# Streams' attention of a two-layer encoder: both head groups in one unit, and W_out prepared beside it

## The reference, cut to what matters

```python
def _mla_attend(q_lat, q_rope, ckv, kr, mask):
    s = (jnp.einsum('bqhl,bkl->bhqk', q_lat, ckv).astype(jnp.float32)
         + jnp.einsum('bqhr,bkr->bhqk', q_rope, kr).astype(jnp.float32)) * MLA_SCALE
    ...
    p = jax.nn.softmax(s, axis=-1).astype(ckv.dtype)
    return jnp.einsum('bhqk,bkl->bqhl', p, ckv)
...
    mix = jnp.concatenate([rms_norm(o_a, g_a), rms_norm(o_swa, g_b)], axis=-1)
    x = layer_norm(ALPHA * x + jnp.einsum('btm,md->btd', mix, w_out), ln1_g, ln1_b)
```

## Time and profile before

| | us |
|---|---|
| median of three runs | 3708.36 (3703.28 to 3713.0) |
| the profiled execution | 3722.36, of which span 3720.5 |
| phase E, layer 0 and layer 1, with its barrier | 197.5 and 196.0 |
| from E's last matmul to the first W_out matmul, layer 0 | 786.7 to 834.9 |
| C from there on | about 147 |
| mean granted TensorE clock of the execution | 0.904 |

### The profile page before, as it was taken

How to read it: one execution, slowest core, us unless ns; L and a number is a source line. 1 busy time by engine, 2 the same in 40 slices (tenths; PEclk the granted TensorE clock), 3 DMA queues, 4 the chain that set the end, 5 groups by cost and what they waited for, 6 DMA issues and landing times. The chain is left out here.

```text
span 3720.5 us, 47086 instructions
## 1 busy us (share of the span) xinstructions
PE 3187.4 (86%) x18498; PEld 2906.4 (78%) x18498; DVE 1675.4 (45%) x3072; ACT 868.9 (23%) x1684; POOL 706.3 (19%) x627
## 2 busy tenths in 40 slices
PE   1978887749899999999859688878598999999995
PEld 1966665747799999999749566657478999999995
DVE  5456775635522322223354577756363322223226
ACT  1323332522311111111123223334223111111111
POOL 1222332001112112211012133310111112121111
PEclk9988897659999999999869789966699999999997
DMA  5320113321211101110133110042322101111001
GB/s 188 100 68 26 29 32 83 101 102 68 70 45 39 39 34 51 39 45 23 49 106 109 50 32 29 24 107 72 112 69 75 40 34 51 40 41 38 34 23 63
DMA packets 118134, 221.32 MB, mean 59 GB/s; under 512 B 33280, under 2 KB 70688, under 8 KB 117296
## 3 DMA queue, kind: packets, MB, share of 16 engines
q1 hardware_dynamic: 106752, 185.43, 15.5%
q0 software_dynamic: 11248, 34.09, 2.4%
HBM read 179.36 MB, written 42.46 MB: 60 GB/s over the span
## 5 line engine op out<-in xcount | busy, mean ns | idle before, releaser
L2131 PE MATMUL PS<-xh,fwh 128*128 128x390 f32 (+1 forms) x2112 | 718.7, 340 | 7.1 <-DVE fwl L2075 7.1
L2132 PE MATMUL PS<-xl,fwh 128*128 128x390 f32 (+1 forms) x2112 | 722.6, 342 | 0.0
L2133 PE MATMUL PS<-xh,fwl 128*128 128x390 f32 (+1 forms) x2112 | 721.8, 342 | 0.0
L2099 DVE TENSOR_TENSOR acc<-acc,PS 128x390 f32<-128x390 f32 x528 | 295.7, 560 | 495.6 <-PE PS L2133 495.6
L2086 DVE TENSOR_TENSOR gate<-PS,gate 128x390 f32<-128x390 f32 x132 | 74.4, 564 | 748.9 <-PE PS L2133 748.9
L2131 PEld LDWEIGHTS PS<-xh,fwh 128*128 128x128 f32 x2112 | 399.0, 189 | 7.8 <-issue 7.3
L2132 PEld LDWEIGHTS PS<-xl,fwh 128*128 128x128 f32 x2112 | 398.8, 189 | 0.6
L2133 PEld LDWEIGHTS PS<-xh,fwl 128*128 128x128 f32 x2112 | 398.2, 189 | 0.0
L2131 PE MATMUL PS<-hidh,fwh 128*128 128x390 f32 (+1 forms) x1056 | 358.4, 339 | 4.5 <-DVE hidl L2090 4.5
L2133 PE MATMUL PS<-hidh,fwl 128*128 128x390 f32 (+1 forms) x1056 | 359.4, 340 | 0.0
L2132 PE MATMUL PS<-hidl,fwh 128*128 128x390 f32 (+1 forms) x1056 | 358.8, 340 | 0.0
(11 more groups left out here) (428 smaller groups left out, 5719.2 us busy)
## 6 DMA issues: line engine op xcount, KB each, us to landing
raw<-in_W_FF SPq DMA_DIRECT2D x88, 512.0 KB, 3.2
fraw<-in_W_FF SPq DMA_DIRECT2D x44, 512.0 KB, 3.2
raw<-in_W_IN SPq DMA_DIRECT2D x16, 592.0 KB, 5.0
ht<-out_H SPq DMA_DIRECT2D x18, 512.0 KB, 4.9
sqt_scratch<-sqTs POOLq DMA_DIRECT2D x18, 512.0 KB, 4.7
mt<-mix_scratch SPq DMA_DIRECT2D x18, 512.0 KB, 4.4
hc<-out_H SPq DMA_DIRECT2D x18, 512.0 KB, 3.5
out_H<-yo POOLq DMA_DIRECT2D x18, 512.0 KB, 2.9
```

Of the source, the lines that this page charges most:

```text
L2099: dve.tensor_tensor(a, a, Tb[e % 2][:, 0:NT[i]], ALU.add).then_inc(S("f_y"), 1)
L2131: pe.matmul(out, wh, mh, start=start, stop=False)
L2132: pe.matmul(out, wh, ml, start=False, stop=False)
L2133: return pe.matmul(out, wl, mh, start=False, stop=stop)
```

## The change

- A unit holds both head groups of a stream: 9 units (8 streams, then meta). Its latent scores fill two banks and its window scores and the last latent columns a third. The turned probabilities are written back into these same banks, so that no banks for turning are needed; the output bank exists twice. The two softmax scales are multiplied into the queries, so that the maximum serves as it is.
- Eleven blocks are turned in three groups for each stream (copies of 512, 512 and 384 columns). The stages of three consecutive units interleave: an iteration n of TensorE is `values(n-2)`, `scores(n+1)`, `turn_probs(n)`.
- GpSimd makes the lo parts `dkl`, `dsh`, `dvl`, `dtl` and `woutl`. VectorE keeps `drs` (32 rows instead of 64) and the casts of `dsh` and `dth`. ScalarE's `dvh` has 1152 columns. The rotary keys are loaded three times instead of four.
- W_OUT is loaded by SyncE during E (part k beside stream k), split by ScalarE and GpSimd, and complete at E's end. The parameters of C, `mt` and `hc` of tile 0 are loaded in E, and its squares, root and `mn` are made there. The store of `mixo` isn't waited for in E.
- W_UK's split, the loads of the queries, and the six cache copies (now issued by SyncE) move to phase B.

```diff
-def plan_units():
...
+                def stream_keys(b):
+                    i = b % 2
+                    sem = S(f"dm_in{i}")
+                    if b == 1:
+                        sp.wait_ge(S("qa"), QN(l, 1) + 1)
+                    if b >= 2:
+                        sp.wait_ge(S("s_done"), U(l, b - 2) + 1)
+                    sp.dma_start(dkraw[i][:, :], CKVT[l, b]).then_inc(sem, 16)
+                    for j in range(3):
+                        sp.dma_start(drraw[i][ROPE * j:ROPE * (j + 1), :], KRT[l, b]).then_inc(sem, 16)
...
+                def stream_values(b):
...
+                    if b >= 2:
+                        sp.wait_ge(S("pv"), U(l, b - 2) + 1)
...
+                def w_out_load(k):
+                    sp.dma_start(woraw[:, k, :], w_out_rows[:, k, :]).then_inc(S("wo_in"), 16)
...
+                keys_lo(0)
+                keys_lo(1)
+                for n in range(UNITS + 2):
+                    if 1 <= n <= NB:
+                        values_lo(n - 1)
+                    if n + 2 < NB:
+                        keys_lo(n + 2)
+                    if n >= 2:
+                        store_window(n - 2)
+                    if n < KD:
+                        w_out_lo(n)
```

More of the change, by code:

```diff
@@ L88, in is_frames @@
     return t < SEQ // P
-def plan_units():
[L92 to L125, removed]
+UNITS = NB + 1
+TURN_GROUPS = 3 * NB + 1
+TAIL = 2 * BANK
+PKEYS = CKEYS + NS
+SKEYS = WKEYS + NS
 HALF = 4
@@ L433, in program @@
[L433 to L466, removed]
+        qrT = [m("qrT8", [96, HEADS * P], F32R), m("qrT9", [96, P], F32R)]
+        qlh = [m("qlh8", [P, HEADS * P], F32R), m("qlh9", [P, P], F32R)]
@@ new lines, in program @@
+        m = Map(wuq_at)
+        dkraw.append(m("dkraw1", [P, CKEYS]))
+        drraw.append(m("drraw1", [96, CKEYS]))
+        dtraw.append(m("dtraw1", [META + NS, 2, P]))
+        dth.append(m("dth1", [META + NS, 2, P], F32R))
+        dsraw.append(m("dsraw1", [P, KVH, WKEYS]))
+        assert m.at <= wuv_at
+        dkl = [Map(wuq_at if i else keys_at + 4 * 4160)(f"dkl{i}", [P, CKEYS], F32R) for i in range(2)]
+        dvl = [Map(pb_at + 2 * 4864 + 4608 * i)(f"dvl{i}", [P, 9, P], F32R) for i in range(2)]
@@ new lines, in q_latent @@
+                def q_latent(i):
+                    r = rows(8 + i)
+                    out = s_of(1) if i == 0 else OO
+                    pe.wait_ge(S("qa_lo"), QN(l, i) + 1)
+                    if i == 1:
+                        pe.wait_ge(S("qa_rope"), QN(l, 1) + 1)
+                    for h in range(HEADS):
+                        p = slice(64 * (h % 2), 64 * (h % 2) + 64)
+                        c0 = P * place_of(h)
+                        ins = three(out[:, c0:c0 + r], wukh[p, h // 2, :], wukl[p, h // 2, :],
+                                    qnh[i][p, h // 2, :], qnl[i][p, h // 2, :], True, True)
+                    ins.then_inc(S("qb"), 1)
@@ new lines, in project @@
+                def project(i):
+                    r = rows(8 + i)
+                    hi, lo = (olh, oll) if i == 0 else ol9
+                    out = s_of(1 - i)
+                    pe.wait_ge(S("out_read"), U(l, NB - 1 + i) + 1)
+                    for h in range(HEADS):
+                        c = slice(h * HD, h * HD + HD)
+                        ins = three(out[0:r, c], hi[:, place_of(h), :], lo[:, place_of(h), :], wuvh[:, c], wuvl[:, c],
+                                    True, True)
+                    ins.then_inc(S("oa"), 1)
```

1017 lines of the change are left out of this document (470 added, 547 removed).

## The result

The changed kernel takes 3590.7 us (median of four runs, 3584.8 to 3595.5) against 3710.7 us before (median of four runs, 3703.3 to 3720.5): 120 us less, ratio 0.967 with an interval of 0.965 to 0.970. The forecast was 3585. The profiled execution has a span of 3590.1 us at a mean clock of 0.918.

The account below looks back on a forecast made before the run. No engine was full in E: TensorE waited for VectorE and ScalarE, much of its work at half clock. Savings of 27 us in E and 35 to W_out, 62 per layer, 124 in all, took 3708.4 to 3585 us, range 3545 to 3632.

Parts of the forecast that it names:

- Start and head: Start of phase E: TensorE starts at 607.2 for 610.5, and the first scores end near 634 instead of 649.5.
- Step: Stream steps of E: five full steps at 14.5 us, 94 us from first to last scores, before 110.9.
- GpSimd beside VectorE: Steps of E: their operations on SBUF exclude each other, adding 1.5 us to the chain of 11.3: 12.8.
- End: End of E, after the last scores: 31 us, for 26.7 before.
- E to W_out: From E's last matmul to the first W_out matmul: 11.5 us for 48.2, saving taken as 35 per layer.
- Loads: Loads in E, W_OUT's parts added: no price, but little slack.
- C: Phase C, from W_out on: as long as before.
- (a): Rival, E: half clock throughout, steps of 16.4 us, 50 us saved per layer, 3608 us; chance 0.20.
- (b): Rival, E: full clock, other queues bound, steps 11.5 to 12 us, 78 saved per layer, 3552 us; chance 0.15.
- (d): Rival, E: slower, GpSimd and VectorE block each other, steps near 23 us, such a case 3725 us; chance 0.04.

Follow-up runs that it names:

- e11_act_order: Changed kernel with ScalarE's hi part of W_OUT moved ahead of the copies of the turned probabilities, instead of behind the exponentials: 3586.4 us, ratio 0.966.
- e3_pool_order: Changed kernel with GpSimd's W_OUT subtraction of each step done one step later, behind the lo parts of values and keys: 3585.6 us, ratio 0.967.
- e9_dkl_on_vector: Changed kernel with the lo part of the latent keys, `dkl`, made by VectorE ahead of `drs` instead of by GpSimd: 3607.4 us, ratio 0.971.
- e6_no_wo_lo: Changed kernel without GpSimd's eight W_OUT subtractions, the hi part used a second time in the product: 3573.0 us, ratio 0.961.

## Why the prediction was right

By its own steps, layer 0 where nothing is said:

- **Start and head.** First matmul at 608.0, predicted 607.2; first maximum at 634.5, predicted near 634.
- **Step: a term mis-sized.** 94 us forecast between the first and the last scores, 90.7 measured. The forecast had five full steps of 14.5 us. The kernel has four: in the seventh no keys are prepared any more (`n + 2 < NB` fails), and it takes 9.6 us. The four take 13.7 us on the mean (13.4 in layer 1). The chain through ScalarE and VectorE, 11.3 us, and 1.5 for GpSimd beside VectorE made 12.8, and 12.9 is what the steps show that TensorE doesn't set. The step of the forecast that failed is the mark-up from 12.8 to 14.5 for all full steps alike, at a mean clock of 0.68. It added TensorE's slowness to the chain, where the longer of the two counts in each step: TensorE fills the step at clock 0.50 (14.84 us, no gap), and the chain sets the one of 12.9; the two others, 13.7 and 13.4, lie between. The second and third maximum came at +14.2 and +12.1 against 9.6 and 12. That the sum came within 3.3 us is in part luck: the first two steps took 4.7 us more than forecast and the seventh 4.9 less.
- **GpSimd beside VectorE.** The hold was put at 1.5 us; `drs` alone is held for 2.2. The sum hit because the links without a hold were shorter than their estimates, 10.6 us for 11.3. That W_OUT has its price in the 14.5 us was right in kind, but its size was not worked out: it is 11.5 us per layer for a saving of 16.
- **End: a term mis-sized.** 34.4 us for 31. By luck this makes up for the steps, 3.4 us against 3.3: E's last matmul ended at 759.6, forecast 759.
- **E to W_out.** 12.1 us for 11.5, by the chain that was named. The undoing of single parts shows what it consists of: copies 8.9, tile 0 with the parameters 10.8, W_OUT 16.
- **Loads.** No price, and at most a small one is there: the run without GpSimd's W_OUT part has all loads and steps of 11.3 us, and the loads and ScalarE's hi part together are the 2 us per layer that it leaves.
- **C.** Forecast as long as before. From the first W_out matmul to the first FFN matmul it takes 2.3 us more in layer 0 and 3.2 in layer 1 (151.1 for 148.8, 151.8 for 148.6). No run here was made for the cause.
- **Rivals.** (a) and (b) are both present: single steps at clock 0.50 with TensorE full, and steps set by the other queues. Mean clock in the steps is 0.68, as before the change, and the 16.4 us that (a) gave to a step was not reached, 14.84 being the longest. (d) is real as a mechanism, 2 to 3 us a step in the changed kernel and 6 in the step of e11_act_order shown above (`sums`, `Pb` and `drs`), and far from 23 us.

The two layers give 64.2 and 63.2 us from B's end to W_out, 127 together, forecast 124. C gives 5.5 of it back, so that 122 are left at the first FFN matmul. The medians differ by 120, the profiled spans by 130. Of these 130, 6 come from phase B of the two profiled executions (before 350.4 and 351.3 us, after 351.0 and 345.0), and that is not the change: B has the same instructions on TensorE in every kernel here, and takes between 340.5 and 351.9 us in the profiles. The windows view of B in the changed kernel, layers 0 and 1, and then in e3_pool_order:

```profile
253.50:604.50 351.00, 302.07 (x2130) 214.67 (x2130) 259.65 (x446) 107.38 (x177) 113.11 (x116) 0.89 0.12 36
2024.00:2369.10 345.10, 297.57 (x2130) 210.19 (x2130) 259.63 (x447) 108.49 (x178) 113.18 (x116) 0.91 0.12 37
```

```profile
253.80:594.30 340.50, 292.65 (x2130) 208.23 (x2130) 259.54 (x446) 107.39 (x177) 113.22 (x116) 0.92 0.13 37
2006.70:2351.70 345.00, 297.61 (x2130) 210.45 (x2130) 259.61 (x446) 108.55 (x178) 113.19 (x116) 0.90 0.13 37
```

2130 matmuls each time; 340.5 us at clock 0.92, 345 at 0.90 to 0.91, 351 at 0.89. The same holds within E: which steps have the clock at 0.50 differs between layers of one kernel. Why an idle TensorE of 2 us is followed by a step at 0.50 in one place and not in another stays open; no run here was made for it.

## What to carry to other kernels

Work out the loop through the in-order queues, link by link, and compare it with the fullest engine, in each step anew: the larger of the two is the step, not their sum. When work goes to an idle GpSimd, look at which VectorE instruction on SBUF will stand in front of it; moving the work shifted the hold to another one here (e11_act_order, e9_dkl_on_vector), and it shrank where GpSimd's operation was taken out of the stretch (e6_no_wo_lo). VectorE's instructions that read PSUM kept their time, but no run moved a held one there. And judge an edit of a few us by the stretch that it touches, since an untouched phase may differ by 10 us from one execution to the next.

## What was not expected of the hardware

- An addition of a single column on VectorE took 1.30 us instead of 0.16, and the 1056-column scaling 2.92 instead of 0.77, beside GpSimd's subtractions; the maxima and the `PTl` copies, which read PSUM, kept 1.26 and 0.67 to 0.69 us throughout.
- GpSimd is held as well: `dtl` 1.73 us beside `drs`, 0.72 alone. And a waiting VectorE instruction can be passed again: `drs` was held through two subtractions in a row, for 4.04 us (1.23 alone).
- An unchanged phase of 351 us was 340.5 us in another execution, with the granted clock at 0.92 instead of 0.89.
